# Three expert blocks fed by transposes of fetched rows, and a fourth split place from the fourth piece

## The reference, cut to what matters

```python
def _hier_moe(h, w_r1, b_r1, w_r2, b_r2, w_gate, w_up, w_down):
    hf = h.reshape(B * T, D)                       # 256 x 1024, normalized
    g_sel = argmax(hf @ w_r1 + b_r1)               # one of 4 groups per token
    # two of the 4 experts of that group, with weights -> combine (256 x 16)
    hid = silu(einsum('nd,edf->nef', hf, w_gate)) * einsum('nd,edf->nef', hf, w_up)
    hid = hid * combine[..., None]
    return einsum('nef,efd->nd', hid, w_down)      # w_gate, w_up: 16 x 1024 x 256
x = x + _hier_moe(_rmsnorm(x, g_ffn), ...)
```

## Time and profile before

| | |
|---|---|
| median of three runs | 1084.66 us |
| the profiled execution | 1084.64 us |
| its span, first to last instruction | 1082.6 us |
| TensorE busy | 1070.2 us (99%) |
| VectorE busy | 726.8 us (67%) |
| ScalarE busy | 617.7 us (57%) |
| GpSimd busy | 50.2 us (5%) |
| mean rate of the DMA engines | 200 GB/s |

### The profile page before, as it was taken

The page is one execution under the profiler, slowest core; times in us unless marked ns, Lnnn a source line. Parts: engine busy times, 40 slices in busy tenths (PEclk is TensorE's granted clock), DMA queues, the critical chain, the costliest instruction groups (busy, mean ns, idle before and its releaser), DMA issues.

```text
span 1082.6 us, 17152 instructions
## 1 busy us (share of the span) xinstructions
PE 1070.2 (99%) x7044; PEld 957.6 (88%) x7044; DVE 726.8 (67%) x814; ACT 617.7 (57%) x731; POOL 50.2 (5%) x41
## 2 busy tenths in 40 slices
PE   9999999999999999999999999999999999999997
PEld 7998889999989999998898777889999978878886
DVE  7954665865766544545765648895455678899995
ACT  7653369674465444443673437775444467877773
POOL 0600100000000000000000000000000002000000
PEclk9999999999999999999999999999999999999999
DMA  8552254554655555555346433434446457999992
GB/s 314 196 187 77 87 183 167 204 211 170 229 179 196 196 194 194 194 192 196 117 156 215 159 98 112 156 120 154 163 161 230 160 200 274 356 378 381 364 402 92
DMA packets 31921, 216.92 MB, mean 200 GB/s; under 512 B 4304, under 2 KB 4560, under 8 KB 6384
## 3 DMA queue, kind: packets, MB, share of 16 engines
q1 hardware_dynamic: 29824, 211.93, 54.9%
q0 software_dynamic: 1616, 2.66, 0.7%
q10 hardware_dynamic: 416, 1.39, 0.3%
HBM read 215.44 MB, written 3.67 MB: 202 GB/s over the span
## 4 chain that ended last, share of the span: by engine, by line
PE 93%; DVE 5%; ACT 1%; issue 1%; DMA 0%; POOLq 0%; DVEq 0%; ACTq 0%
PE bank L567 28%; PE bank L569 28%; PE bank L568 27%; PE bank L628 2%; DVE wlo L1642 1%; PE bank L1039 1%; PE bank L961 1%; PE bank L943 1%; DVE last_lo L1642 1%; DVE wlo L1645 1%; PE bank L709 0%; PE bank L688 0%; PE bank L874 0%; PE bank L1091 0%; PE bank L706 0%
## 5 line engine op out<-in xcount | busy, mean ns | idle before, releaser
L1645 DVE TENSOR_TENSOR wlo<-raw,whi 128x2048 fp32r<-128x2048 f32 x138 | 317.7, 2307 | 167.8 <-ACT whi L1125 167.6
L1125 ACT ACTIVATE whi<-raw 128x2048 fp32r<-128x2048 f32 (+1 forms) x168 | 319.4, 1906 | 134.9 <-PE bank L569 132.7
L567 PE MATMUL bank<-normedT_hi,whi 128*128 128x256 f32 x640 | 177.6, 278 | 0.0
L568 PE MATMUL bank<-normedT_lo,whi 128*128 128x256 f32 x640 | 177.0, 277 | 0.0
L569 PE MATMUL bank<-normedT_hi,wlo 128*128 128x256 f32 x640 | 177.0, 276 | 0.0
L1125 ACT ACTIVATE buf<-bank 128x512 f32<-128x512 f32 (+5 forms) x147 | 70.9, 526 | 156.7 <-PE bank L569 128.1
L567 PE MATMUL bank<-xT_hi,whi 128*128 128x256 f32 (+1 forms) x448 | 127.1, 284 | 0.8 <-issue 0.8
L568 PE MATMUL bank<-xT_lo,whi 128*128 128x256 f32 (+1 forms) x448 | 126.3, 282 | 0.0
L569 PE MATMUL bank<-xT_hi,wlo 128*128 128x256 f32 (+1 forms) x448 | 126.3, 282 | 0.0
L567 PEld LDWEIGHTS bank<-normedT_hi,whi 128*128 128x128 f32 x640 | 120.2, 188 | 1.0 <-issue 0.6
L568 PEld LDWEIGHTS bank<-normedT_lo,whi 128*128 128x128 f32 x640 | 120.2, 188 | 0.7 <-issue 0.2
(11 more groups left out here) (396 smaller groups left out, 2227.1 us busy)
## 6 DMA issues: line engine op xcount, KB each, us to landing
raw<-weights_dram SPq DMA_DIRECT2D x175, 1024.0 KB, 5.0
buf<-weights_dram SPq DMA_DIRECT2D x24, 1024.0 KB, 8.0
buf<-x_dram SPq DMA_DIRECT2D x2, 512.0 KB, 4.1
buf<-mem_dram ACTq DMA_DIRECT2D x1, 1024.0 KB, 8.9
token_rows<-buf SPq DMA_DIRECT2D x1, 1024.0 KB, 8.6
buf<-final_w_dram POOLq DMA_DIRECT2D x1, 512.0 KB, 3.8
con<-consts_dram SPq DMA_DIRECT2D x1, 486.0 KB, 8.8
buf<-small_w_dram SPq DMA_DIRECT2D x1, 432.0 KB, 11.4
```

The source lines that it names most:

```text
L567: E.matmul(out_, lh, rh, start=start, stop=False)
L568: E.matmul(out_, lh, rl, start=False, stop=False)
L1125: return S.activation(out_, in_, func, **kw)
L1645: V.tensor_tensor(wlo[:, n % SLOTS, :], raw[:, n % SLOTS, :], whi[:, n % SLOTS, :].bitcast(f32), sub).then_inc(piece_split, 1)
```

## The change

Feature tiles of blocks 2 to 4 are no longer gathered with `PICK`. TensorE transposes the fetched rows `OWN[2..4]` instead, three transposes of 128 x 128 for each k, into the same banks `xb.k`. This is done in passes 4, 5 and 6 (k = 0 to 2, 3 to 5, 6 and 7) behind `expert_up`, and the high and low copies move with it. The row fetches of blocks 2, 3, 4 are issued ahead of those of 0 and 1 and count on a semaphore of their own. The fourth split place, which had to wait for the last gather, is used from piece 3 on (before: from piece 12, the second of pass 4).

```diff
-FOURTH = AT[1, 4]
+FOURTH = SLOTS
+REST = {4: range(0, 3), 5: range(3, 6), 6: range(6, KT)}
...
-            def gather_rest(first, last):
-                pe.wait_ge(slotted, 2)
-                for k in range(first, last):
-                    gather(begin(f"xb.{k}")[:, 0:3 * P], k, 2 * P, SLOTTED).then_inc(gathered, 1)
+            def rest_turned(p):
+                pe.wait_ge(rest_gathered, 16 * 3)
+                for k in REST[p]:
+                    b = begin(f"xb.{k}")
+                    for i in range(3):
+                        last = E.transpose(b[:, i * P:(i + 1) * P], OWN[2 + i][:, k * P:(k + 1) * P], ident)
+                    last.then_inc(gathered, 1)
...
             spread_slots()
-            gather_rest(0, 2)
             expert_turn(0)
             for p in range(1, PASSES):
                 expert_up(p)
-                if p <= 3:
-                    gather_rest(2 * p, 2 * p + 2)
+                if p in REST:
+                    rest_turned(p)
                 expert_down(p - 1)
                 expert_turn(p)
...
                     if u == FOURTH:
-                        act.wait_ge(gathered, 4 + KT)
+                        act.wait_ge(gathered, 4)
                     else:
                         act.wait_ge(pieces_used, n + 1 - (SLOTS if u < FOURTH else 4))
...
             for p in range(PASSES):
-                if p in (1, 2, 3):
+                if p in REST:
                     expert_silu(p)
-                    rest_high(2 * p, 2 * p + 2)
+                    rest_high(p)
                 if p + 1 < PASSES:
                     feed(act, M0 + AT[1, p + 1])
-                if p not in (1, 2, 3):
+                if p not in REST:
                     expert_silu(p)
-                if p == 0:
-                    rest_high(0, 2)
...
-                    dve.wait_ge(rows_gathered, 16 * BLOCKS)
+                    dve.wait_ge(rows_gathered, 16 * 2)
...
-            rest_low(0, 2)
             hidden_low(0)
...
-                if p <= 5:
+                if p <= max(REST):
                     expert_hidden(p)
                 if p + 1 < PASSES:
                     feed(dve, M0 + AT[1, p + 1])
-                if p > 5:
+                if p > max(REST):
                     expert_hidden(p)
-                if p <= 3:
-                    rest_low(2 * p, 2 * p + 2)
+                if p in REST:
+                    rest_low(p)
...
-            for blk in range(BLOCKS):
+            for blk in (2, 3, 4, 0, 1):
                 pool.indirect_dma_start(OWN[blk], None, token_rows, ...)\
-                    .then_inc(rows_gathered, 16)
+                    .then_inc(rest_gathered if blk >= 2 else rows_gathered, 16)
```

More of the change, by code:

```diff
@@ L345, in program @@
         rows_stored, tokens_ready, rows_gathered = sem("rows_stored"), sem("tokens_ready"), sem("rows_gathered")
+        rest_gathered = sem("rest_gathered")
         out_row = sem("out_row")
@@ L1601, in _, with rest_high @@
             feed(act, M0 + 2)
-            def rest_high(first, last):
-                for k in range(first, last):
+            def rest_high(p):
+                for k in REST[p]:
                     act.wait_ge(gathered, 4 + k + 1)
@@ L2295, in expert_hidden, with rest_low @@
                 V.scalar_tensor_tensor(HDM, SLM, share[:, min(p // 4, GROUPS), p % 4:p % 4 + 1], banks[6][:, 256:512], mult, mult).then_inc(moe_hid, 1)
-            def rest_low(first, last):
-                for k in range(first, last):
+            def rest_low(p):
+                for k in REST[p]:
                     dve.wait_ge(xb_high, k + 1)
```

## The result

The changed kernel took 1087.40 us, median of 21 runs (1085.10 to 1089.27), the kernel before 1083.85 us, median of 21 runs on the same chip (1082.85 to 1086.49). The ratio is 1.0030, 95% interval 1.0024 to 1.0036: 3.5 us slower, a small change that the interval still tells from none. The forecast was 1085.8 with a range to 1088.3. The time is inside the range, but it is the time of rival 2 (1086.6 to 1087.5), not of the case that was called likeliest. As a difference it is larger than either: +1.1 was forecast and +1.9 to +2.8 for rival 2, both counted from 1084.66, while the kernel before has its median at 1083.85 here.

A forecast was written before the change was run, and what follows sets the result against it. TensorE, 99% busy, bounds the kernel, VectorE nearly so. Gathers -4.23, transposes +2.75, today's turn 6 lateness -1.5, loads +0.9, new stalls +3.6 give +1.5; +1.1, between load cases, gives 1085.8 us, range 1082.6 to 1088.3.

The forecast's parts named there:

- rival 2: Gap before turn 0: TensorE's clock falls, +1.7 us, partly covered by late loads; 1086.6 to 1087.5 us; chance 0.17.
- the case that was called likeliest: Whole kernel: the main forecast, +1.1 us, 1085.8 us, chance 0.54.
- Gathers removed: Passes 1 to 3 on TensorE: eight gather matmuls, 1.41 us each time, leave its line; 4.23 us saved.
- the gather of pass 0: Before turn 0: removing it saves nothing, as turn 0 waits for slot spread, silu and hidden product.
- Transposes: Behind expert_up 4, 5 and 6 on TensorE: 24 added at 0.114 us each, 2.75 us in all.
- Rival 3: Passes 4 to 6: transposes cost their length, 0.27 us each, up to 1088.5 us; chance 0.10, shared with later loads.
- Late loads: Turns 2 and 3: pieces 9 and 12 land no sooner, stalls of 0.5 and 0.4 us; bounds 0 and 0.9.
- The walk of passes 4 to 7: Turns 5 to 7: ScalarE's and VectorE's work followed by durations gives stalls of 1.2, 0.2 and 2.2 us.
- The stall of turn 5: Turn 5: ScalarE's and VectorE's serial 14.4 us against TensorE's 13.27 makes TensorE wait 1.2 us.
- The sum: Turn 7: comes at 973.55 against 972.08, +1.5 us with late loads, +0.6 with loads that keep up.
- The step that failed: Gap before turn 0: argument against rival 2, clock 1.00 from 904 to 907.3 us, gather filling less than half.
- Rival 1: Passes 4 to 7: stalls do not build up, sum -3.0 us, 1081.7 us; chance 0.15.

The follow-up runs named there:

- x1: Changed kernel with six 512-column filler matmuls in the gap before turn 0, results unused; 1086.60 us, 1.0025 of the kernel before.
- x4: x1 with the fourth split place in use from piece 12 again, as in the kernel before; 1086.57 us, ratio 1.0021.
- z1: The changed kernel as it is, timed once more; 1088.42 us, 1.0042 of the kernel before.
- y1: x3 without the filler matmuls, so the gap before turn 0 is open; 1082.61 us, ratio 0.9984.
- x3: x1 plus VectorE's hidden product before the next low part everywhere, ScalarE's high part before silu and copies in passes 4 to 6; 1080.45 us, 0.9966.
- z3: Changed kernel with VectorE's hidden product ahead of the next piece's low part in all passes, gap before turn 0 open; 1084.38 us, 1.0007.
- y2: x3 with 13 unread transposes of the identity as filler in place of the six matmuls; 1081.35 us, ratio 0.9972.
- z2: x3 with the row fetches of blocks 0 and 1 issued later, at 928.2 and 931.6 us; 1080.97 us, ratio 0.9970.

## Why the prediction was right or wrong

- *Gathers removed, 4.23 us.* Right: passes 2 and 3 take 8.43 us each, and pass 1 takes 8.48 in x1, where the clock is up. That the gather of pass 0 saves nothing was right too: turn 0 waits for VectorE, with 1.63 us of idle time for the forecast's 1.6.
- *Transposes, 0.114 us each.* Right: 1.02 us for nine. Rival 3 is out.
- *Late loads, 0.5 at turn 2 and 0.4 at turn 3.* Of the right size in sum, at one place: 0.83 us at turn 3 with the clock up (x1), none at turn 2. In the changed kernel itself the low clock hid it, as rival 2 had it.
- *The walk of passes 4 to 7.* It had 40.2 us from turn 3 to turn 7; after has 40.07, x1 40.18. The stall of turn 5 was forecast as 1.2 us on the hidden product; it is 1.06 us on `own_added`, one product sooner, in the same chain. The one of turn 7 was to be 2.2 us; it is 1.72, and 0.2 in the product before. There is none at turn 6. The items listed for turn 5 add up to 14.6 us and not to 14.4, so that by its own terms the forecast should have been 0.2 higher.
- *The sum, +1.5 with late loads.* x1, which has the stalls and not the clock, has +1.47. The forecast took +1.1, the middle between late loads and loads that keep up; the loads were late.
- *The step that failed* is the one in which the clock stays up: "Against it: the clock is 1.00 from 904 to 907.3 today, and the gather fills less than half of that". That cover was real. With the gather gone TensorE has twelve matmuls of at most 12 columns and then 1.63 us of nothing, and the clock fell in four profiles of four. The price of one fall was right (+1.65, for 1.7), and so was that the late loads cover a part of it (0.57 net). Two things were not in the forecast at all: that a run has more than one fall, since the hole before turn 7 can bring one as well (x4, z1), and that the kernel before has one in every second run, which puts its median between two steps. That 1087.40 lies where rival 2 put it is in part luck: as a difference rival 2 was 0.7 us or more short, for want of these further falls, and the base of 1084.66, 0.8 too high, made up for it. The same holds for the range: the difference of 3.55 is just inside the 3.6 that it allowed.

Rival 1, that the stalls do not build up, would have been right with other orders on ScalarE and VectorE: its 1081.7 lies between y1 and x3.

x3_fill_both beats both kernels: 0.34% faster than before (0.22 to 0.46%, six runs).

## What to carry to other kernels

Price not only the work that leaves TensorE but what stands in its place: a short gap of 1.6 us cost as much again behind it, through the clock, and six throwaway matmuls or thirteen transposes that nobody reads kept the clock up. But look at what comes up next: here a late load took back two thirds of that gain, until two row fetches were moved as well. Where work is moved to later passes, write out the order on the two feeding engines instruction by instruction: the same amount of work in another order made 3.7 us here (x1 to x3), and 0.9 more in the plain passes behind. And take the gaps between groups of run times as a hint: they have the size of whole falls of the clock, and a median hides how many.

## What the runs showed of the hardware

- A whole fall of the clock lasts 3.3 to 3.4 us at 1.2 GHz, behind idle times of 1.63 us (four profiles), 1.70 us (x4) and 1.72 us (z1), and makes what follows late by 1.59 to 1.65 us, by 1.35 us in z3, where part of it lies in idle time. Behind the hole before turn 7 it came in two profiles of four; at 123 us it came with TensorE busy throughout (before). It began 1.1 us behind the end of the gap in the changed kernel's profile, and 0.5 us ahead of it in z3's.
- Transposes at 0.11 us from start to start keep the clock at 1.00 as matmuls do (y2).
- Two indirect row fetches among the 1 MB weight loads, issued at 913.6 and 915.8 us, made the pass of 934 us late by 0.8 us (x3); issued at 928.2 and 931.6 us they made nothing late (z2).
